# Two networks' blocks on one core: a second routing with one scan and an early two-block product, and a final norm set under the last expert block

## The reference, cut to what matters

```python
def hierarchical_moe(h, ...):            # 32 experts in 4 groups of 8, top 2 of the best group
    g_idx = argmax(h @ w_rg + b_rg)                      # the group of each token
    top_val, top_loc = top_k(e_logits[g_idx], 2)
    gates = softmax(top_val) * g_gate
    expert = g_idx * 8 + top_loc
    # assignments are sorted by expert; each expert's list is padded to blocks of 128 rows
    # a block: xb = h[tok]; y = (silu(xb @ w_gate[e]) * (xb @ w_up[e])) @ w_down[e]
    # y * gate is added to its tokens' rows
x = x + gate_f * hierarchical_moe(h, ...)
return rms_norm_2(x, final_g)            # x * rsqrt(mean(x*x) + eps) * final_g
```

## Time and profile before

| what | value |
|---|---|
| median of 3 runs | 2179.3 us (2179.16 to 2180.51) |
| profiled execution, its own time | 2180.93 us |
| its span, first to last instruction | 2179.3 us |
| granted TensorE clock, mean over the span | 0.973 |
| PE, DVE, ACT, POOL busy | 93%, 77%, 57%, 21% of the span |
| last output stage ends, second routing starts on VectorE | 1468.5 us |
| first expert matmul of the second block loop | 1505.0 us |
| last matmul | 2144.1 us |
| DMA over the span | 592.47 MB, 272 GB/s |

### The profile page before, as it was taken

The page is one execution under the profiler, slowest core; times in us unless marked ns, Lnnn a source line. Parts: engine busy times, 40 slices in busy tenths (PEclk is TensorE's granted clock), DMA queues, the critical chain, the costliest instruction groups (busy, mean ns, idle before and its releaser), DMA issues.

```text
span 2179.3 us, 32240 instructions
## 1 busy us (share of the span) xinstructions
PE 2030.7 (93%) x9821; PEld 1685.3 (77%) x9821; DVE 1672.9 (77%) x1890; ACT 1240.9 (57%) x1460; POOL 467.9 (21%) x367
## 2 busy tenths in 40 slices
PE   3999999969999999999699999999999999999993
PEld 2888888857888878787577787888888888878872
DVE  5676755478999999999545455447999999999994
ACT  4311103207878787877533533223888888888873
POOL 2000001101011111111100353110344443433443
PEclk9999999959999999999899999999999999999997
DMA  9277754528999999999711112345999999999994
GB/s 344 89 249 242 244 189 165 198 102 317 381 378 389 380 387 381 386 382 385 262 44 47 41 39 106 126 174 192 395 382 383 376 370 379 377 374 365 367 333 155
DMA packets 234180, 592.47 MB, mean 272 GB/s; under 512 B 23938, under 2 KB 61078, under 8 KB 234108
## 3 DMA queue, kind: packets, MB, share of 16 engines
q1 hardware_dynamic: 207808, 518.06, 63.8%
q0 software_dynamic: 22640, 61.31, 9.6%
q10 hardware_dynamic: 3660, 12.17, 1.5%
HBM read 560.57 MB, written 50.91 MB: 281 GB/s over the span
## 4 chain that ended last, share of the span: by engine, by line
PE 50%; DMA 23%; DVE 11%; SPq 6%; issue 5%; ACT 3%; POOL 1%; ACTq 0%; DVEq 0%; POOLq 0%
PE ps L2156 15%; PE ps L2159 14%; PE ps L2157 14%; DMA ring<-in_w_expert_up 13%; DMA ring<-in_moe_w_down 7%; SPq L534 5%; DVE mL L2043 2%; DVE mL L1646 2%; DMA ring<-in_ada_w 1%; ACT mH L1292 1%; PE ps L2291 1%; PE ps L2435 1%; DVE xz L1792 1%; PE ps L2164 1%; PE ps L2253 1%
## 5 line engine op out<-in xcount | busy, mean ns | idle before, releaser
L2043 DVE TENSOR_TENSOR mL<-ring,mH 128x1024 fp32r<-128x1024 f32 x384 | 480.0, 1291 | 25.1 <-ACT mH L1292 24.4
L1646 DVE TENSOR_TENSOR mL<-ring,mH 128x1024 fp32r<-128x1024 f32 x384 | 454.8, 1222 | 33.8 <-ACT mH L1107 25.2
L1107 ACT ACTIVATE mH<-ring 128x1024 fp32r<-128x1024 f32 x384 | 402.2, 1063 | 100.8 <-PE ps L2159 61.2
L1292 ACT ACTIVATE mH<-ring 128x1024 fp32r<-128x1024 f32 x384 | 398.6, 1058 | 64.7 <-DMA ring<-in_w_expert_up 32.1
L2156 PE MATMUL ps<-mH,xsH 128*128 128x512 f32 x1072 | 428.7, 400 | 4.1 <-DVE mL L2043 2.4
L2159 PE MATMUL ps<-mH,xsL 128*128 128x512 f32 x1072 | 419.3, 391 | 0.0
L2157 PE MATMUL ps<-mL,xsH 128*128 128x512 f32 x1072 | 417.4, 389 | 0.0
L2156 PEld LDWEIGHTS ps<-mH,xsH 128*128 128x128 f32 x1072 | 201.6, 188 | 44.0 <-issue 3.3
L2159 PEld LDWEIGHTS ps<-mH,xsL 128*128 128x128 f32 x1072 | 201.2, 188 | 43.7
L2157 PEld LDWEIGHTS ps<-mL,xsH 128*128 128x128 f32 x1072 | 201.7, 188 | 38.7
L2156 PE MATMUL ps<-mH,hidH 128*128 128x512 f32 x536 | 213.6, 399 | 9.9 <-DVE hidL L1691 7.4
(11 more groups left out here) (419 smaller groups left out, 3187.2 us busy)
## 6 DMA issues: line engine op xcount, KB each, us to landing
ring<-in_w_expert_gate SPq DMA_DIRECT2D x140, 512.0 KB
ring<-in_w_expert_up SPq DMA_DIRECT2D x140, 512.0 KB
ring<-in_w_expert_down SPq DMA_DIRECT2D x140, 512.0 KB
ring<-in_moe_w_gate SPq DMA_DIRECT2D x128, 512.0 KB
ring<-in_moe_w_up SPq DMA_DIRECT2D x128, 512.0 KB
ring<-in_moe_w_down SPq DMA_DIRECT2D x128, 512.0 KB
ring<-in_ada_w SPq DMA_DIRECT2D x96, 512.0 KB
ring<-in_sc_w_in SPq DMA_DIRECT2D x24, 512.0 KB
```

What stands on the lines that cost most here:

```text
L1107: act.activation(mH[:, m % WSETS, :], ring[:, m % RING, :], ACT.Copy).then_inc(S["m1_hi"], 1)
L1292: act.activation(mH[:, wset, :], ring[:, slot, :], ACT.Copy).then_inc(S["m2_hi"], 1)
L1646: dve.tensor_tensor(mL[:, m % WSETS, :], ring[:, m % RING, :], mH[:, m % WSETS, :].bitcast(F32), ALU.subtract).then_inc(S["m1_lo"], 1)
L2043: dve.tensor_tensor(mL[:, wset, :], ring[:, slot, :], mH[:, wset, :].bitcast(F32), ALU.subtract).then_inc(S["m2_lo"], 1)
```

## The change

- **One scan.** Experts take the column `4 * l + g` (g the group, l the place in it), so that blocks of different groups follow each other. `hot32[:, 2]` and `slotm[:, 0]` are laid out by expert and then tile, and one scan over 256 elements, set to zero at each expert by `segs`, replaces the memset and the eight additions. As it counts the own tile too, the triangle becomes `trix = tri - 1`. Three more instructions on GpSimd make `segs` and `trix`. Four small instructions on VectorE turn a column number into the expert's number.
- **An early product for two blocks.** Flags and token numbers of blocks 0 and 1 alone (`early`, 4 columns) are multiplied first, and `tok_in` for both is written from it. The gathers no longer wait for `rows_known`. The table of 47 blocks follows in two products: flags and tokens (96 columns), and gates (48 columns, float32).
- **fp32r tables.** `in_slot`, `early` and `in_block` are float32r, in `mH`. `in_gate` stays float32 in `xz`. `oblk` moves (to `xz` parts 3 and 4; these lines and the declarations are not shown below). The filler counts are 33 for 40, 25 for 44 and none for 26.
- **Overflow.** VectorE takes the output of the block before at its chunk 5, with gate and `gate_ffn_row` in one instruction (`weigh`), copies the row numbers, and waits for `ov_sent`, which GpSimd gives behind the scatter. ScalarE's scaling and GpSimd's copy and multiplication go.
- **Norm.** All eight tiles of `x3_dram` are loaded into ring slots 0 to 7 once the last but one block's scatter has landed, before the last block's output exists, then squared, normed and stored. The last block's rows are gathered from `x3_dram` by GpSimd (`last_base`), added to its weighted output on VectorE, normed as a ninth tile, and scattered into `out` once the eight stores have landed.

```diff
+    x_rows = [ring[:, t, :] for t in range(NT)]
+    sq_rows = [ring[:, NT + u, :] for u in range(RING - NT)]
+    last_rows, last_base = ys[0], xz[:, 7, :]
...
-        overflow_blocks(sp, overflow)
-        sp.wait_ge(S["last_out"], 16)
+        blocks = overflow_blocks(sp, overflow)
+        sp.wait_ge(m2_out[0], 16 * (E2 // 2) + XS_PAST)
+        sp.wait_ge(m2_out[1], 16 * blocks + 16 * (E2 // 2 - 1) + XS_PAST)
+        settle(sp)
         for t in range(NT):
+            sp.wait_ge(S["m2_lo"], 12 * blocks + 12 * (E2 - 1) + t + 1 + past["m2_lo"])
+            settle(sp)
             sp.dma_start(x_rows[t], x3_tiles[:, t, :]).then_inc(x_in[t], 16)
         for t in range(NT):
             sp.wait_ge(S["final_done"], t + 1)
-            sp.dma_start(out.rearrange("(t p) d -> p t d", p=P)[:, t, :], one_rows[t]).then_inc(x_in[t], 16)
+            sp.dma_start(out.rearrange("(t p) d -> p t d", p=P)[:, t, :], x_rows[t]).then_inc(x_in[t], 16)
...
-        pool.wait_ge(S["rows_known"], 2)
...
-            pool.wait_ge(m2_out[1], 16 * (E2 // 2 - 1) + XS_PAST)
-            pool.wait_ge(m2_out[0], 16 * b + 16 * (E2 // 2) + XS_PAST)
+            pool.wait_ge(m2_out[0], 16 * (E2 // 2) + XS_PAST)
+            pool.wait_ge(m2_out[1], 16 * b + 16 * (E2 // 2 - 1) + XS_PAST)
             settle(pool)
-            pool.wait_ge(S["m2_lo"], 12 * b + 12 * E2 + 11 + past["m2_lo"])
+            pool.wait_ge(S["m2_dst"], b + E2)
             settle(pool)
-            pool.tensor_copy(tok_out[0][:], row_of[:, bass.ds(b + (E2 - 1), 1)]).then_inc(S["m2_row"], 1)
-            gate_rows(gated, ys[1], slice(0, D))
-            pool.wait_ge(S["m2_row"], 2 * b + 3 * (E2 - 1) + 2)
-            settle(pool)
-            scatter_rows(gated, tok_out[0]).then_inc(m2_out[0], 16)
+            scatter_rows(ys[1], tok_out[1]).then_inc(m2_out[1], 16)
+            pool.sem_inc(S["ov_sent"], 1)
         blocks = overflow_blocks(pool, overflow)
-        pool.wait_ge(m2_out[1], 16 * (E2 // 2 - 1) + XS_PAST)
-        pool.wait_ge(m2_out[0], 16 * blocks + 16 * (E2 // 2) + XS_PAST)
+        pool.wait_ge(m2_out[0], 16 * (E2 // 2) + XS_PAST)
+        pool.wait_ge(m2_out[1], 16 * blocks + 16 * (E2 // 2 - 1) + XS_PAST)
         settle(pool)
-        pool.tensor_copy(last_tok[:], row_of[:, bass.ds(blocks + (E2 - 1), 1)]).then_inc(S["m2_row"], 1)
-        for half in range(2):
-            pool.wait_ge(S["last_y"], half + 1)
-            gate_rows(ys[0], ys[0], slice(512 * half, 512 * half + 512))
-        pool.wait_ge(S["m2_row"], 2 * blocks + 3 * (E2 - 1) + 3)
+        pool.wait_ge(S["m2_dst"], blocks + E2)
         settle(pool)
-        scatter_rows(ys[0], last_tok).then_inc(S["last_out"], 16)
+        pool.indirect_dma_start(out=last_base, out_offset=None, in_=x3_dram,
+                                in_offset=bass.IndirectOffsetOnAxis(ap=last_tok[:, 0:1], axis=0),
+                                bounds_check=T - 1, oob_is_err=False).then_inc(S["last_in"], 16)
+        for i in range(NT + 1):
+            pool.wait_ge(S["var_final"], i + 1 + past["var_final"])
+            own = stat_of(i)
+            pool.tensor_tensor(own[2], own[1], neghalf[:, 0:1], ALU.pow).then_inc(S["rstd_final"], 1)
         for t in range(NT):
-            pool.wait_ge(S["var_final"], t + 1 + past["var_final"])
-            pool.tensor_tensor(stat[:, 10, t:t + 1], stat[:, 9, t:t + 1], neghalf[:, 0:1], ALU.pow).then_inc(S["rstd_final"], 1)
+            pool.wait_ge(x_in[t], 64)
+        pool.wait_ge(S["last_done"], 1)
+        pool.indirect_dma_start(out=out, in_=last_rows, in_offset=None,
+                                out_offset=bass.IndirectOffsetOnAxis(ap=last_tok[:, 0:1], axis=0),
+                                bounds_check=T - 1, oob_is_err=False).then_inc(S["last_out"], 16)
+        pool.wait_ge(S["last_out"], 16)
...
-                if c == 6:
-                    act.wait_ge(S["m2_used"], 12 * b + used)
-                    act.wait_ge(m2_out[1], 16 * (E2 // 2 - 1) + XS_PAST)
-                    act.wait_ge(S["m2_row"], 2 * b + 3 * (E2 - 1))
-                    settle(act)
-                    act.activation(ys[1].rearrange("p (a b) -> p a b", a=2), ps[:, 4:6, :], ACT.Copy,
-                                   scale=slot_w[:, bass.ds(b + (E2 - 1), 1)]).then_inc(S["ov_y"], 1)
...
-        act.wait_ge(m2_out[0], 16 * (E2 // 2) + XS_PAST)
-        act.wait_ge(S["m2_used"], 12 * blocks + 12 * E2 + past["m2_used"])
+        act.wait_ge(S["m2_lo"], 12 * blocks + 12 * E2 + past["m2_lo"])
         settle(act)
-        for half in range(2):
-            act.activation(ys[0][:, 512 * half:512 * half + 512], ps[:, 4 + half, :], ACT.Copy,
-                           scale=slot_w[:, bass.ds(blocks + (E2 - 1), 1)]).then_inc(S["last_y"], 1)
-        for t in range(NT):
-            act.wait_ge(x_in[t], 48)
-            act.activation(two_rows[t], x_rows[t], ACT.Square,
-                           accum_out=stat[:, 8, t:t + 1]).then_inc(S["sq_final"], 1)
+        for i, t in enumerate(FINAL_ORDER):
+            if i >= len(sq_rows):
+                act.wait_ge(S["sq_final"], i - len(sq_rows) + 1 + past["sq_final"])
+            if t < NT:
+                act.wait_ge(x_in[t], 48)
+            else:
+                act.wait_ge(S["last_y"], 1)
+            act.activation(sq_rows[i % len(sq_rows)], x_rows[t] if t < NT else last_rows, ACT.Square,
+                           accum_out=stat_of(i)[0]).then_inc(S["sq_final"], 1)
...
-                steps.mark(dve.tensor_tensor(hot32[:, i, :, 8 * g:8 * g + 8], hot8[:, i],
+                steps.mark(dve.tensor_tensor(hot32[:, i, :, bass.ds(g, 8, step=4)], hot8[:, i],
                                              hot4[:, :, g:g + 1].to_broadcast([P, NT, 8]), ALU.mult))
         steps.wait()
-        step(dve.tensor_tensor(hot32[:, 2], hot32[:, 0], hot32[:, 1], ALU.add))
-        step(dve.memset(slotm[:, 0, 0, :], 0.0))
-        for t in range(1, NT):
-            step(dve.tensor_tensor(slotm[:, 0, t, :], slotm[:, 0, t - 1, :], hot32[:, 2, t - 1, :], ALU.add))
-        dve.tensor_tensor(cnt[:, 5, :], slotm[:, 0, NT - 1, :], hot32[:, 2, NT - 1, :], ALU.add).then_inc(S["hot_ready"], 1)
+        step(dve.tensor_tensor(by_tile(hot32[:, 2]), hot32[:, 0], hot32[:, 1], ALU.add))
+        dve.wait_ge(S["route_consts"], 8 + past["route_consts"])
+        dve.tensor_tensor_scan(in_line(slotm[:, 0]), segs[:].rearrange("p e t -> p (e t)"), in_line(hot32[:, 2]),
+                               0.0, ALU.mult, ALU.add).then_inc(S["hot_ready"], 1)
...
+        step(flags(early, 2))
+        steps.mark(times(early[:, :, 0, :], early, tokid[:], 2))
         for i in range(2):
+            if i == 1:
+                steps.wait()
             dve.tensor_tensor(in_slot[:, NT * i:NT * i + NT, :], iota_s[:].unsqueeze(1).to_broadcast([P, NT, P]),
                               by_expert(place[:, 0, i, :], P), ALU.is_equal).then_inc(S["onehots"], 1)
+        step(flags(in_block, NBLK + 1))
+        dve.wait_ge(S["tok_tr"], 1 + past["tok_tr"])
...
+        step(dve.tensor_copy(tokc[:], ps[:, 1, 64:66]))
+        def tokens2(e, r):
+            first = static(e) and e < 2
+            dve.tensor_copy(tok_in[r][:], (tokc if first else row_of)[:, bass.ds(e, 1)]).then_inc(S["m2_tok"], 1)
+        tokens2(0, 0)
+        tokens2(1, 1)
+        times(in_block[:, :, 0, :], in_block, tokid[:], NBLK + 1).then_inc(S["onehots"], 1)
+        times(in_gate, in_block, r2[:, 8:10, :], NBLK + 1).then_inc(S["onehots"], 1)
...
-        steps.mark(dve.tensor_copy(bexp_u[:, 0, 0:NBLK], bexp[:, 0:NBLK]))
+        step(dve.tensor_copy(bexp_u[:, 0, 0:NBLK], bexp[:, 0:NBLK]))
+        step(dve.tensor_scalar(bexp_u[:, 1, 0:NBLK], bexp_u[:, 0, 0:NBLK], 3, None, ALU.bitwise_and))
+        step(dve.tensor_copy(bgrp[:], bexp_u[:, 1, 0:NBLK]))
+        step(dve.scalar_tensor_tensor(out=bexp[:, 0:NBLK], in0=bgrp[:], scalar=31.0, in1=bexp[:, 0:NBLK], op0=ALU.mult,
+                                      op1=ALU.add))
+        steps.mark(dve.tensor_scalar(bexp_u[:, 0, 0:NBLK], bexp[:, 0:NBLK], 0.25, None, ALU.mult))
...
+        def weigh(dst, block):
+            return dve.scalar_tensor_tensor(out=dst.rearrange("p (a b) -> p a b", a=2), in0=ps[:, 4:6, :],
+                                            scalar=slot_w[:, bass.ds(block, 1)],
+                                            in1=gate_ffn_row[:].rearrange("p (a b) -> p a b", a=2),
+                                            op0=ALU.mult, op1=ALU.mult)
...
+                if c == 5:
+                    dve.wait_ge(S["m2_used"], 12 * b + 12 * E2 + past["m2_used"])
+                    dve.wait_ge(m2_out[1], 16 * b + 16 * (E2 // 2 - 1) + XS_PAST)
+                    dve.tensor_copy(tok_out[1][:], row_of[:, bass.ds(b + (E2 - 1), 1)]).then_inc(S["m2_dst"], 1)
+                    weigh(ys[1], b + (E2 - 1)).then_inc(S["ov_y"], 1)
+                    dve.wait_ge(S["ov_sent"], b + 1)
...
```

(41 more changed lines are left out.)

91 lines of the change are left out of this document (47 added, 44 removed).

## The result

The changed kernel takes 2183.58 us in the median (2182.51 to 2186.72), the kernel before 2179.47 beside it: ratio 1.0017, interval 1.0011 to 1.0023. I had forecast 2171.3. The profiled execution of the changed kernel has a span of 2181.6, 2.3 above that of before.

The account below looks back on a forecast made before the run. TensorE and DMA were both taken to be at their limit in the second block loop, so only its start and what follows could move. -6.7 + 4.9 - 6.2 = -8.0 from 2179.3 gave 2171.3 us, range 2167 to 2180.

Parts of the forecast that it names:

- Routing, -6.7 forecast: First term, routing ahead of the second block loop: first split and block 1's request come earlier, -6.7 us.
- TensorE does 16 table products of one pass (2.1) and 16 gate products of two passes (4.1) from 1488.1, and is done at 1494.3: Routing: TensorE's products ahead of block 0's transposes, so VectorE splits at 1495.5 instead of 1502.24.
- Fewer filler matmuls cost nothing while products follow within 2 us: Routing on TensorE: cutting the filler was claimed to have no cost.
- My bound of -5.0: Routing term's smallest gain: strided ranks, and gate products slower by half, -5.0 us.
- both limits of the loop move together: Second block loop: TensorE and DMA limits start earlier by the same amount, so all of -6.7 us counts.
- Turns, +4.9 forecast: Second term, overflow turns: VectorE's copy, weigh and wait add 2.6, 1.0 and 1.3 us, +4.9 in all.
- So `ov_sent` should come about 1.1 us behind `weigh`: Overflow turns: GpSimd's increment comes soon after weigh, for a sum per turn of 2.55 us.
- The rival of the held VectorE: Overflow turns: increment follows the scatter's 1.61 us, each of three turns costs 1.5 more, 2175.7 us; chance 0.17.
- The falling clock at each hidden product: Overflow turns: longer pauses put turns 0 and 1 at half clock, +8.0 us, 2179.3; chance 0.07.
- End, -6.2 forecast: Third term, from the last down product to the end: 34.8 us against 41.0, -6.2 us.
- 0.8 and 4.14, and 0.3 to the end: Kernel's end: last scatter into out after tile 7's store, its landing, then the finish, at M + 34.8.
- The third rival: Norm gains little or TensorE's products hold the first split: 4 us of gain go, 2175.3 us; chance 0.12.

Follow-up runs that it names:

- e2: Changed kernel with 40 filler pairs in place of 33 ahead of the ranks and 6 behind the early product; 2180.54 us, ratio 1.0003 to the kernel before.
- e14: e2 with one fp32 product of 144 columns for tokens, flags and gates, and 10 filler pairs behind the early product; 2179.05 us, ratio 0.9997.
- e1: Changed kernel without VectorE's wait for ov_sent behind weigh; median 2177.84 us, ratio 0.9993 to the kernel before.
- e4: Kernel before with only the routing part of the change (scan, early product, tables, expert list, gathers ahead of rows_known); ratio 0.9989.
- e7: Changed kernel with the filler of e2 and without VectorE's wait for ov_sent; 2171.82 us, ratio 0.9967 to the kernel before.
- e8: e7 with the wait for the last scatter's landing moved from GpSimd's queue to SyncE's; 2170.73 us, ratio 0.9962 to the kernel before.
- e11: e4 with the filler of e2, so old turns and old end; 2173.74 us, ratio 0.9969 to the kernel before.
- e9: Changed kernel with the weigh step and its wait for ov_sent at VectorE's chunk 8 in place of chunk 5; ratio 1.0015 to the kernel before.
- e10: e8 with the weigh step and its wait for ov_sent at chunk 8; 2178.76 us, ratio 0.9996 to the kernel before.
- e3: Changed kernel without the last scatter into out and its wait, so rows of out lack the last block's part; ratio 1.0002 to the kernel before.
- e6: Changed kernel with the wait for the last scatter's landing moved from GpSimd's queue to SyncE's; ratio 1.001 to the kernel before.
- e16: e4 with the filler of e2 and one fp32 product, so old turns and end; 2172.11 us, ratio 0.9965 to the kernel before.
- e15: e8 with one fp32 product in place of the separate table and gate products; 2169.80 us, ratio 0.9957 to the kernel before.

## Why the prediction was wrong

**Routing, -6.7 forecast, -3.4 measured.** The step that failed is "TensorE does 16 table products of one pass (2.1) and 16 gate products of two passes (4.1) from 1488.1, and is done at 1494.3". At full clock they take 1.99 and about 3.7 (the estimate from `e2`), so the sizes were right; they ran at half: 3.65 and 7.02, from 1490.42, done at 1500.9. Shown by `e2` (start of the loop 4.9 us sooner) and `e14` (6.7 sooner). 2.3 of the lateness are ahead of the tables: strided ranks (1.17 and 1.10 against 0.60 and 0.59), and VectorE's 1.52 us of waiting for the early product, 0.35 where the filler ahead of it ran at full clock. "Fewer filler matmuls cost nothing while products follow within 2 us" failed too: the pause was 1.69 us, and the clock fell 2.1 us behind it, which it did in `e1` as well and in none of the eight executions that were at full at R and made no pause. It made the filler behind it slow, and the 1.52 long. VectorE's own steps were right (scan 0.69, flags and tables as forecast). My bound of -5.0 had no row at half clock in it, though the earlier trace rows shows one. That VectorE waits for TensorE's table was the first of my signs of being wrong, and it came. The assumption that both limits of the loop move together failed as well: the stream started 4.45 earlier and the matmuls 0.6 later, and 3.4 of the stream's lead reached the end of the loop.

**Turns, +4.9 forecast, +7.5 measured.** "So `ov_sent` should come about 1.1 us behind `weigh`" holds in turns 1 and 2 and fails in turn 0, where the GpSimd queue waits for block 30's scatter first. I named what is queued behind the waiting instruction on VectorE, and not what stands ahead of the increment on GpSimd; and I had the landing at 4.14, read at the quiet end, for a scatter that lands in 9.64 under the stream. `e1` shows 6.0 us for that wait in turn 0, 0.8 and 1.0 in turns 1 and 2. Turn 1 of before held 1.6 us of half clock (20.44 against 18.85 in `e4`), which did not recur; this hid the wait of turn 1. The rival of the held VectorE is refuted: it resumes at 2093.07, ahead of the scatter's start on the engine at 2093.16. The falling clock at each hidden product didn't come in the changed kernel: its clock was low from 2090.9 to 2097.7, from within TensorE's 6.04 us of idling on, and full again at the down product of 2103.05. A fall in turn 0's down product came in `e7`, `e8`, `e11` and, with larger pauses, in `e9` and `e10`.

**End, -6.2 forecast, -1.9 measured.** The steps up to the start of the last scatter are right within 1.5 us: squares at M + 5.2 for 6.6, tile 7 multiplied at M + 25.5 for 25.4, the ninth row at M + 27.2 for 27.0, the last store landed at M + 28.1 for 29.6. "0.8 and 4.14, and 0.3 to the end" is the step that failed: 2.4 us of landing, then 7.1 of drain. It stood in the profile before, 7.77 us long, hidden by 0.9 us behind SyncE's last store; the change made GpSimd's queue the last to finish. `e3` and `e6` show it.

**The other rivals.** The order of experts costs nothing that can be seen: the loop is 3.9 us shorter, at 374 GB/s as before. The third rival is nearest to what came: it has a norm that gains little and TensorE's products holding the first split, but it priced them at 4 us, named another cause for the norm, and left the turns as they were.

**Open.** What brings the clock down at R + 21, and why only where it had been low shortly before: the coincidence over fifteen executions speaks for the early product, but only the fall at R + 25 was taken apart by edits. With the low clock at R it cost `e16` 2.2 us of its loop start against `e15` (32.21 and 30.01), 1.3 of it ahead of the early product. What holds the scatter up without VectorE's wait is open too. Why the loop of `e10` took 565.72 was not tried.

## What to carry to other kernels

When a queue becomes the last to finish, look at what its engine does behind its last instruction: here 7 us of GpSimd's closing were hidden as long as another queue was later. When an engine is made to wait for another's increment, go through all that stands ahead of the increment in that queue, in the first turn above all, where it still waits for what ran under the full stream. Count TensorE's narrow products at both clock levels: splitting one product of 144 columns (4.19) into 96 and 48 cost about 1.5 us at full clock, by the estimate from `e2`, and 6.5 at the half clock that came with it. And one trace shows one execution: compare what the clock had done before the stretch before a difference in the stretch is put down to the edit.

## What the runs showed of the hardware

- GpSimd's closing drain ends 7.0 to 7.1 us behind its last engine instruction or wait, with or without an indirect DMA ahead of it, and whether or not that DMA has landed (before, `e3`, `e6`, after).
- An indirect scatter of 128 rows occupied GpSimd for 1.6 to 1.7 us in the block loop, for 2.58 to 2.60 in the changed turns with VectorE's wait, and without it for 8.05 to 8.25 in six of eight cases in turns 1 and 2 and for 2.57 in two. VectorE's subtractions ran beside the turns' scatters in all of these kernels and beside the loop's last one, so they alone don't explain the long ones.
- An accumulating scatter of 128 rows landed 9.64 us after its start under the weight stream, against 4.14 with the DMA engines otherwise idle.
- TensorE's clock fell to 1.2 GHz while the engine was busy without a pause, in the gate products of 48 columns behind those of 96 (`e2`); behind 32 matmuls of 144 columns it stayed at 2.4 (`e14`).
- The same code had two histories of the clock: a short fall 250 us ahead of R and full clock at R in ten executions, no such fall and half clock at R in eight.
